# Two more Strassen quads and two fewer ordinary tile pairs in each SwiGLU input projection, with the preparation on VectorE and ACT in a new order

## The reference

```python
def swiglu(h, w_in, w_out):
    g, u = jnp.split(h @ w_in, 2, axis=-1)
    return (jax.nn.silu(g) * u) @ w_out
...
        x = x + rms_norm(m, g[1])
        f = swiglu(rms_norm(x, g[2]), ffn_w_in[li], ffn_w_out[li])
        x = x + rms_norm(f, g[3])
```

## Time and profile before

| | us |
|---|---|
| median of 3 runs | 1508.47 (1508.04 to 1508.66) |
| profiled execution | 1508.73 |
| its span, first to last instruction | 1507.2 |
| TensorE busy | 1498.5 |
| TensorE weight loads busy | 1481.2 |
| VectorE busy | 968.6 |
| ACT busy | 689.6 |
| POOL busy | 214.2 |

### The profile page before, as it was taken

The page is one execution under the profiler, slowest core; times in us unless marked ns, Lnnn a source line. Parts: engine busy times, 40 slices in busy tenths (PEclk is TensorE's granted clock), DMA queues, the critical chain, the costliest instruction groups (busy, mean ns, idle before and its releaser), DMA issues.

```text
span 1507.2 us, 27754 instructions
## 1 busy us (share of the span) xinstructions
PE 1498.5 (99%) x10922; PEld 1481.2 (98%) x10922; DVE 968.6 (64%) x1350; ACT 689.6 (46%) x1131; POOL 214.2 (14%) x173
## 2 busy tenths in 40 slices
PE   9999999999999999999999999999999999999998
PEld 8999999999999999999999999999999999999998
DVE  6454577667344588777764438889588877755444
ACT  5244432324343444655553435286563555554433
POOL 0100033333000002121110000505002111210002
PEclk9999999999999999999999999999999999999999
DMA  7322232322222212423332323212222333333211
GB/s 242 106 74 72 76 110 79 96 86 90 82 84 84 84 44 71 112 83 111 84 110 83 95 68 94 85 44 91 87 60 85 84 96 99 83 99 98 82 60 68
DMA packets 171568, 133.55 MB, mean 89 GB/s; under 512 B 4920, under 2 KB 149584, under 8 KB 171348
## 3 DMA queue, kind: packets, MB, share of 16 engines
q1 hardware_dynamic: 169812, 128.30, 28.5%
q0 software_dynamic: 1664, 3.95, 1.0%
HBM read 128.92 MB, written 3.29 MB: 88 GB/s over the span
## 4 chain that ended last, share of the span: by engine, by line
PE 98%; DVE 1%; ACT 0%; DMA 0%; issue 0%; SPq 0%; POOLq 0%; POOL 0%; ACTq 0%
PE ps L568 97%; DVE hl L1875 0%; PE ps L634 0%; DMA wide<-in_x_prompt_dram 0%; ACT hh L1312 0%; DVE wlo L1887 0%; DVE yb L1812 0%; POOLq L81 0%; POOL xT L2293 0%; PE ps L1029 0%; PE ps L718 0%; DVE acc L1554 0%; DVE hl L1577 0%; ACT whi L1054 0%; DVE wide L1915 0%
## 5 line engine op out<-in xcount | busy, mean ns | idle before, releaser
L568 PE MATMUL ps<-hh,whi 128*128 128x288 f32 x2624 | 642.5, 297 | 0.0
L568 PE MATMUL ps<-hh,wlo 128*128 128x288 f32 x2624 | 637.5, 295 | 0.0
L568 PE MATMUL ps<-hl,whi 128*128 128x288 f32 x2624 | 637.5, 295 | 0.0
L568 PEld LDWEIGHTS ps<-hh,whi 128*128 128x128 f32 x2624 | 446.7, 188 | 2.2 <-DVE wlo L1537 0.2
L568 PEld LDWEIGHTS ps<-hh,wlo 128*128 128x128 f32 x2624 | 447.5, 188 | 0.0
L568 PEld LDWEIGHTS ps<-hl,whi 128*128 128x128 f32 x2624 | 447.4, 188 | 0.0
L1054 ACT ACTIVATE whi<-stage 128x1024 fp32r<-128x1024 f32 (+2 forms) x176 | 174.4, 999 | 377.8 <-PE ps L568 377.8
L1537 DVE TENSOR_TENSOR wlo<-stage,whi 128x1024 fp32r<-128x1024 f32 (+2 forms) x176 | 208.6, 1190 | 205.3 <-ACT whi L1054 205.0
L568 PE MATMUL ps<-eh,whi 128*128 128x288 f32 x512 | 151.6, 296 | 0.3 <-DVE wlo L1887 0.3
L568 PE MATMUL ps<-el,whi 128*128 128x288 f32 x512 | 151.1, 295 | 0.0
L568 PE MATMUL ps<-eh,wlo 128*128 128x288 f32 x512 | 150.6, 294 | 0.0
(11 more groups left out here) (201 smaller groups left out, 1562.7 us busy)
## 6 DMA issues: line engine op xcount, KB each, us to landing
stage<-in_ffn_w_in_dram SPq DMA_DIRECT2D x88, 512.0 KB, 4.0
stage<-in_ffn_w_out_dram SPq DMA_DIRECT2D x40, 512.0 KB, 3.9
stage<-in_gm_w_in_dram SPq DMA_DIRECT2D x32, 384.0 KB, 3.5
stage<-in_gm_w_in_dram SPq DMA_DIRECT2D x24, 512.0 KB, 3.8
stage<-in_gm_w_out_dram SPq DMA_DIRECT2D x24, 512.0 KB, 3.8
stage<-in_rg_w_in_dram SPq DMA_DIRECT2D x16, 512.0 KB, 3.8
stage<-in_rg_w_out_dram SPq DMA_DIRECT2D x8, 512.0 KB, 3.9
wide<-in_x_prompt_dram SPq DMA_DIRECT2D x4, 512.0 KB, 7.1
```

What stands on the lines that cost most here:

```text
L568: return pe.matmul(out, w, x, start=start, stop=stop, skip_group_check=more)
```

## The change

NR goes from 3 to 2, so each FI stage has two rounds of four ordinary units (four tile pairs) and NQ = 18 quads. The third round's splits, evictions, SiLUs and gates go. The preparation of the quads on VectorE and ACT is written in a new order around what is left, the low half of part 6 moves behind low b(1) in the first quad step, and the sums of quad 1 move behind low a(1). TensorE's, POOL's and SyncE's programs change only by NR and NQ. Line numbers after the change are lower by 4 to 6 on VectorE.

```diff
--- before.py
+++ after.py
@@ -63,7 +63,7 @@
     def slot(n):
         return slot_of[n]
 
-    NR = 3
+    NR = 2
     NQ = KF - 2 * NR
 
     def seq(n):
@@ -1405,43 +1405,37 @@
                 silu(name, 0, 1)
                 split_hi(n + 6)
                 split_hi(n + 7)
-                silu(name, 1, 0)
-                split_hi(n + 8)
-                silu(name, 1, 1)
                 act.wait_ge(comb_ready, C0 + 1)
                 part_hi_of(layer, 0, quarter(hn, 0, 0))
                 part_hi_of(layer, 1, quarter(hn, 0, 1))
-                split_hi(n + 9)
-                act.wait_ge(comb_ready, C0 + 2)
-                part_hi_of(layer, 2, sraw_of(0))
-                split_hi(n + 10)
-                silu(name, 2, 0)
-                act.wait_ge(comb_ready, C0 + 3)
-                part_hi_of(layer, 3, sraw_of(1))
-                split_hi(n + 11)
                 act.wait_ge(unit_done, seq(L0 - 3))
                 product_hi("a", 0, layer, 0)
                 product_hi("a", 0, layer, 1)
-                silu(name, 2, 1)
+                act.wait_ge(comb_ready, C0 + 2)
+                part_hi_of(layer, 2, sraw_of(0))
+                silu(name, 1, 0)
+                act.wait_ge(comb_ready, C0 + 3)
+                part_hi_of(layer, 3, sraw_of(1))
+                silu(name, 1, 1)
                 act.wait_ge(unit_done, seq(L0 - 2))
                 product_hi("b", 0, layer, 0)
                 product_hi("b", 0, layer, 1)
                 act.wait_ge(unit_done, seq(L0 - 1))
                 product_hi("c", 0, layer, 0)
                 product_hi("c", 0, layer, 1)
+                copy_p1(0, layer)
+                product_hi("a", 1, layer, 0)
+                wait_product("P2", 0, layer)
+                product_hi("a", 1, layer, 1)
                 act.wait_ge(unit_done, seq(L0))
                 act.wait_ge(comb_ready, C0 + 5)
                 part_hi_of(layer, 4, sraw_of(3))
-                copy_p1(0, layer)
+                copy_q5(0, layer)
                 part_hi_of(layer, 5, quarter(hn, 1, 1))
-                product_hi("a", 1, layer, 0)
-                wait_product("P2", 0, layer)
-                product_hi("a", 1, layer, 1)
+                copy_u2(0, layer)
+                product_hi("d", 0, layer, 0)
+                part_hi_of(layer, 6, sraw_of(2))
                 silu_c11(0, layer)
-                product_hi("d", 0, layer, 0)
-                copy_q5(0, layer)
-                part_hi_of(layer, 6, sraw_of(2))
-                copy_u2(0, layer)
 
                 quad_step(name, 0)
                 with act.Fori(0, LOOP) as i:
@@ -1934,6 +1928,8 @@
                 if q > 0:
                     c12(q - 1, layer, i)
                 product_lo("b", q + 1, layer, i)
+                if q == 0:
+                    part_lo_of(layer, 6, sraw_of(2))
                 product_lo("d", q + 1, layer, i)
                 c22(q, layer, i)
                 if not out:
@@ -1978,34 +1974,25 @@
                 ffn_evict(name, 1, 0, g0)
                 combine(2, sraw_of(1), ALU.add, quarter(hn, 0, 1))
                 ffn_evict(name, 1, 1, g0)
-                split_lo(n + 8)
-                combine(3, quarter(hn, 0, 0), ALU.subtract, quarter(hn, 1, 0))
                 part_lo_of(layer, 0, quarter(hn, 0, 0))
+                part_lo_of(layer, 1, quarter(hn, 0, 1))
+                sums_1_3(0, layer)
                 ffn_evict(name, 1, 2, g0)
-                part_lo_of(layer, 1, quarter(hn, 0, 1))
-                split_lo(n + 9)
-                ffn_evict(name, 1, 3, g0)
-                part_lo_of(layer, 2, sraw_of(0))
-                split_lo(n + 10)
-                sums_1_3(0, layer)
-                ffn_evict(name, 2, 0, g0)
-                part_lo_of(layer, 3, sraw_of(1))
-                split_lo(n + 11)
                 sums_2_4(0, layer)
                 product_lo("a", 0, layer)
-                ffn_evict(name, 2, 1, g0)
+                part_lo_of(layer, 2, sraw_of(0))
                 product_lo("b", 0, layer)
-                ffn_evict(name, 2, 2, g0)
+                combine(3, quarter(hn, 0, 0), ALU.subtract, quarter(hn, 1, 0))
+                ffn_evict(name, 1, 3, g0)
+                part_lo_of(layer, 3, sraw_of(1))
+                product_lo("c", 0, layer)
+                product_lo("a", 1, layer)
+                part_lo_of(layer, 4, sraw_of(3))
+                c11(0, layer)
                 sums_1_3(1, layer)
-                product_lo("c", 0, layer)
+                part_lo_of(layer, 5, quarter(hn, 1, 1))
                 sums_2_4(1, layer)
-                ffn_evict(name, 2, 3, g0)
-                part_lo_of(layer, 4, sraw_of(3))
-                part_lo_of(layer, 5, quarter(hn, 1, 1))
-                c11(0, layer)
-                product_lo("a", 1, layer)
                 product_lo("d", 0, layer)
-                part_lo_of(layer, 6, sraw_of(2))
 
                 quad_step(name, 0)
                 with dve.Fori(0, LOOP) as i:
```

## The result

| | us |
|---|---|
| before, median of 5 runs | 1508.66 (1508.04 to 1508.78) |
| changed, median of 5 runs | 1524.66 (1524.41 to 1525.35) |
| ratio, with its 95% interval | 1.0108 (1.0094 to 1.0122) |
| changed, profiled execution and its span | 1525.35, 1523.8 |

The changed kernel is slower by 16.0 us. The prediction was 1521.0 with a range of 1512 to 1525.

A forecast was written before the change was run, and what follows sets the result against it. TensorE's matmuls bound the kernel, with VectorE saturated where quads begin. New idle 9.8 us a layer, less 0.3 of old hand-over and 3.24 gained, gave +6.2, +12.4 for two layers: about 1521 us, range 1512 to 1525.

The forecast's parts named there:

- its bound of 7 us: Upper bound for the load of quad 2 after low d(0), taken as 6.0 us with bounds 4.5 to 7.
- the 0.4 us a layer: Margin added above the upper end of the two unknowns, 1524.3 us, to reach the range's end of 1525.
- TensorE's gain: Four ordinary units out, two quads in: 3.24 us a layer won, 6.48 in all, if quads find their data.
- Steps 1 to 3: VectorE's queue at the first quads makes P1(0) 2.9, P6(0) 0.8 and P1(1) 1.6 us late.
- The gates: POOL's two gating multiplies ahead of low d(0) slow VectorE: 0.9 us each, at most 1.23.
- Step 4: ACT's copy of P7(0), queued behind high b(1), which waits for VectorE's sum, makes P4(0) 2.2 us late.
- the six waits: New TensorE idle time at the first quads: 2.9, 0.8, 1.6, 2.2, 1.4 and 0.9, 9.8 us a layer.
- Step 5: Quad 2's load waits for low d(0) and takes 6.0 us; P1(2) is 1.4 and P7(1) 0.9 us late.
- rival C: TensorE's granted clock falls as a cost of its own: 2.5 us a layer; chance 0.04.
- A: VectorE's preparation for the first quads stays hidden, P1(0) starts at 574.13: 1502.0 us; chance 0.06.
- B: POOL's multiplies cost VectorE nothing and the load lands early: +2.9 us a layer, 1514.3 us; chance 0.13.
- D: An unseen stall, an ACT copy late in every quad: 0.5 us over 36 quads, 1540 us; chance 0.03.

The follow-up runs named there:

- prepared_ahead: Changed kernel with VectorE's last two tile splits made earlier, scaling, last eviction, SiLUs and gates deferred into quads, first steps reordered: 1502.93 us.
- u7_early: Changed kernel with ACT's copy of P7(0) moved ahead of the high part of b(1): 1524.92 us.
- filled_gaps: Changed kernel with 36 small unused matmuls a layer put ahead of the five matmuls that TensorE waits for: 1524.54 us.
- gates_small: Changed kernel with POOL's two second-round multiplies in each layer cut from 576 to 8 columns: 1520.09 us.
- new_order_nr3: Three rounds of ordinary tiles as in the kernel before, with the changed kernel's preparation order behind them: 1520.24 us.
- splits_d_u7: Changed kernel with last two tile splits before the RMS-factor wait, d(0) behind c(0), P7(0) copied ahead of high b(1): 1513.55 us.

## Why the prediction was right, and where it was short

**How near it was.** The way and the mechanism were right, the size was short: 12.5 us were forecast and 16.0 measured, and 1524.66 lies 0.34 us inside the upper end, with two of the five runs above it. The load in layer 1 went beyond its bound of 7 us and the second gate to its bound, so that the range held owes something to luck: to the 0.4 us a layer that had been put on top without a row. (The terms of the sum as written make +6.26 us a layer, not +6.2.)

**TensorE's gain, right.** 48 matmuls went, and prepared_ahead cashes 5.8 of the 6.5 us.

**Steps 1 to 3, right in kind.** P1(0) was to wait 2.9 us and waits 2.92 and 3.00. P1(1) was to start at 585.8 and starts at 586.3 on that scale. P6(0), foreseen 0.8 late, has no wait in layer 0: the clock was low from 576.8 to 580.2, TensorE took the time over P1 and P2 instead, and the wait was spent in slow matmuls. In layer 1, where it stayed full there, P6(0) waits 0.50 and P1(1) 1.73 (foreseen 1.6).

**The gates, mis-sized.** The term was 0.9 each, from the mean of a pair; they measured 1.09 and 1.24, as the upper bound (1.23) had it. That is 0.5 a layer. The pair of before was 0.58 and 1.23, and both cases here, like the first round's two, are nearer the larger.

**Step 4, right in place, wrong in weight.** P4(0) was to be 2.2 late for ACT's copy, and waits 1.98. But u7_early shows that this wait had no price of its own as long as the load of quad 2 was behind it: the time only came back at the next start. Summing the six waits was right since each was counted in the order in which it falls, with all earlier ones behind it. To read one of them as what its repair would win would have been wrong.

**Step 5, mis-sized.** The load was to take 6.0 from low d(0), as in the row of before. It took 6.9 and 7.6. The DMA itself had 6.04 and 6.76 of it; the rest is SyncE's queue. This is the term with the largest error, 0.9 and 1.6 us. An estimate of 4.4 us stood beside it, by the Trainium skill, DMA: Bandwidth & Descriptors, section Anatomy of one DMA. That section's fit is of DMAs issued from GpSimd, and these loads are issued by SyncE. The chain has 6.04 and 6.76 us, and the measured durations decide.

**The clock, left out.** I gave it 0.04 as a case of its own (rival C). It did fall, in three stretches. In layer 0 it cost nothing (filled_gaps). In layer 1 the third stretch lies behind the load of quad 2, when little is late any more; there filled_gaps is 0.8 us shorter in its profile (582.47 us between the two activation table loads below, 583.25 in the changed kernel). 0.2 of it is there before the slow stretch, when P1(2) starts, from a shorter load; 0.7 is there at P7(1), right behind that stretch. This is one pair of executions, and the medians of the two kernels differ by 0.1, so the clock's share, some 0.5 us, is an estimate. As a term of the sum it was worth under 1 us, where C had 2.5 a layer.

**The sum.** A mark for each layer's length is an activation table load of ACT, one ahead of FI0, one behind its quads and one behind those of FI1. In the changed kernel:

```profile
366.35 1.28 ACT L1222 ACT_TABLE_LOAD   x1
...
787.03 1.28 ACT L1222 ACT_TABLE_LOAD   x1
...
1370.28 1.28 ACT L1222 ACT_TABLE_LOAD   x1
```

Before, they are at 366.59, 779.61 and 1353.81 us. So layer 0 came out 420.68 - 413.02 = 7.66 us longer where 6.2 were foreseen; 0.5 for the gates and 0.9 for the load are 1.4 of the 1.5. Layer 1 is 583.25 - 574.20 = 9.05 longer: 0.5, 1.6 and some 0.8 left, of which the clock may have 0.5; the rest isn't placed. The two layers make 16.7 us, and the two profiled executions are 16.6 apart.

**What was to be seen.** VectorE was to be busy without a gap until 595 and then wait about 3 us: it waits 3.50 us from 595.4 on. TensorE was to wait about 20 us in some twelve pieces: it waits 17.1 in ten, and the rest went into slow matmuls.

**The rivals.** A, that preparation is hidden, fell at its decision point: P1(0) did not start at 574. Its time, 1502.0, is what prepared_ahead reaches (1502.9) once the work is really taken out. The Trainium skill, Perfetto Trace Analysis, section Identifying the Most-Contended Engine, would look to the engine with the highest occupancy, and judges TensorE by its weight loads, 97% here; the engine that limited had 65%. B, that POOL's multiplies cost VectorE nothing and the load lands early, is refuted by gates_small and by the load's 6.9 and 7.6 us. D, a stall in every quad, has no row.

## What to carry to other kernels

An engine that is busy 64% of the kernel can be the bound in the 30 us that matter; cut its busy time by stretch before shortening what runs beside it. Work on one engine can be the cover for another's: before taking it out, count what stands behind it on the other engines, move out of that stretch whatever nobody needs yet, and only then cash the gain. Of several waits in a row, mending one alone may win nothing (u7_early, 0 us) and the same edit 3.6 us once the next link is mended.

## What the runs showed of the hardware that I had not expected

**The price of a multiply on POOL.** A 128x576 POOL multiply of 1.7 to 2.4 us lengthened the VectorE instruction beside it by 0.86 to 1.24 us; with 8 columns in place of 576 the effect is gone. The rows of the changed kernel fit an exclusion better than a sharing. POOL's multiply starts at 581.35, while VectorE is in this part, which isn't lengthened:

```profile
581.09 1.34 DVE L1869 TENSOR_TENSOR el<-wide,eh 128x1152 fp32r<-128x1152 f32 x1
```

POOL takes 2.38 us, where the shortest of its multiplies in the quads of prepared_ahead take 1.42 and 1.44; 1.42 from the part's end is 583.85, and POOL ends at 583.73. The next low part of VectorE, from 582.36, is the long one and ends at 584.82, 1.1 us behind POOL, which is about its own length of 1.22. The Trainium skill, SBUF — State Buffer, section SBUF: two separate sides, states it so: a VectorE operation with two SBUF inputs and a GpSimd operation that reads SBUF share a pair of ports, which one of them holds for its whole instruction. The trace agrees, with a price of 0.86 to 1.24 us for a multiply.

**The granted clock isn't a matter of the gap's length alone.** In layer 0 of the changed kernel it fell to the lower level for about 3.4 us after P1(0) had waited 2.92 us, and again after P4(0) had waited 1.98. In layer 1 P1(0) waited 3.00 us and P4(0) 1.98, and it fell behind neither, only behind the 2.74 of P1(2). new_order_nr3 has the same wait of 1.98 in both layers, with the clock at 1.00 from 570 to 630 us in layer 0, and at a mean of 0.97 from 1140 to 1200 in layer 1, where it is below 1.00 only behind that wait. splits_d_u7 waits 2.34 us at P1(1) and keeps 1.000 in all. And in the 5 us of the tail that the earlier trace rows show, TensorE was busy only 2.68 us at full clock. I had drawn from that last row that gaps of this size are harmless, and they weren't.

**The same load takes different times.** From low d(0) to the sums that wait for it: 6.0 us before, 6.9 and 7.6 after, of which the DMA has 6.04 and 6.76; the median over all 88 loads of 512 KB of these weights is 4.2 us from issue to landing. Two quads' loads then move 304 GB/s between 595 and 600. What makes it longer in layer 1 stays open; no run was made for it.
